# Twenty merge gates move from the attention into the merge, and the weight pieces get a fourth place

## The reference

```python
h = x * (1.0 + scale) + shift                     # ada: modulation from the condition
a_q, a_k, a_v, a_g, g_q, ..., s_u, s_v, s_g, m_a, m_g, m_s = split(h @ w_in)
y_attn = blocked_attention(q, k, v) * silu(a_g)   # softmax attention, 8 heads of 64
y_gla  = rms_norm(gla_scan(...) both ways) * silu(g_g)   # gated linear attention, 4 heads
y_sgu  = s_u * (w_s @ layer_norm(s_v) + b_s) * silu(s_g)
m = (sigmoid(m_a) * (y_attn @ w_br_attn)
     + sigmoid(m_g) * (y_gla @ w_br_gla)
     + sigmoid(m_s) * (y_sgu @ w_br_sgu))
x_new = layer_norm(alpha * x + gate * (m @ w_out))
```

## Time and profile before

| | us |
|---|---|
| median of 3 runs | 1342.85 (1341.75 to 1343.16) |
| profiled execution, whole | 1345.98 |
| span of the profiled execution, first to last instruction | 1344.1 |
| mean granted clock of PE in the profiled execution | 0.986 of full speed |

### The profile page before, as it was taken

The page is one execution under the profiler, slowest core; times in us unless marked ns, Lnnn a source line. Parts: engine busy times, 40 slices in busy tenths (PEclk is TensorE's granted clock), DMA queues, the critical chain, the costliest instruction groups (busy, mean ns, idle before and its releaser), DMA issues. The chain is left out here.

```text
span 1344.1 us, 19268 instructions
## 1 busy us (share of the span) xinstructions
PE 1299.5 (97%) x7922; PEld 990.2 (74%) x7922; DVE 625.0 (46%) x1096; ACT 552.3 (41%) x908; POOL 61.5 (5%) x88
## 2 busy tenths in 40 slices
PE   5999999999999999999999999999999999999996
PEld 2767778776778888878878889997767566666663
DVE  2313765576443352567476685767213252222212
ACT  2447433644663132346755568441344211111112
POOL 0000010232000000000000230000000000000000
PEclk7899999999999999999999999999899999999999
DMA  9523022235332341323432313553323869999990
GB/s 383 219 110 141 32 95 95 94 126 194 152 125 94 114 157 44 134 100 123 158 147 103 119 39 126 220 192 109 125 107 136 317 234 411 396 421 403 414 369 34
DMA packets 34653, 239.05 MB, mean 178 GB/s; under 512 B 4480, under 2 KB 4736, under 8 KB 6656
## 3 DMA queue, kind: packets, MB, share of 16 engines
q1 hardware_dynamic: 34560, 237.74, 45.5%
HBM read 236.68 MB, written 1.05 MB: 177 GB/s over the span
## 5 line engine op out<-in xcount | busy, mean ns | idle before, releaser
L231 DVE TENSOR_TENSOR pieces_lo<-weight_ring,pieces_hi 128x1024 fp32r<-128x1024 f32 x156 | 192.5, 1238 | 241.1 <-ACT pieces_hi L223 240.1
L249 PE MATMUL proj<-h_hi,pieces_hi 128*128 128x512 f32 (+1 forms) x800 | 284.7, 356 | 4.1 <-DVE pieces_lo L231 2.1
L251 PE MATMUL proj<-h_hi,pieces_lo 128*128 128x512 f32 (+1 forms) x800 | 276.1, 345 | 0.0
L250 PE MATMUL proj<-h_lo,pieces_hi 128*128 128x512 f32 (+1 forms) x800 | 274.7, 343 | 0.0
L223 ACT ACTIVATE pieces_hi<-weight_ring 128x1024 fp32r<-128x1024 f32 x156 | 163.5, 1054 | 147.2 <-PE score L251 96.1
L249 PEld LDWEIGHTS proj<-h_hi,pieces_hi 128*128 128x128 f32 x800 | 151.0, 189 | 31.6 <-issue 11.7
L250 PEld LDWEIGHTS proj<-h_lo,pieces_hi 128*128 128x128 f32 x800 | 151.4, 189 | 22.2 <-issue 2.9
L251 PEld LDWEIGHTS proj<-h_hi,pieces_lo 128*128 128x128 f32 x800 | 151.0, 189 | 19.8
L2042 PE MATMUL turn<-expert_parts,e_gathered 128*64 128x256 f32 x768 | 85.3, 379 | 0.8 <-DVE e_gathered L2234 0.8
L2042 PEld LDWEIGHTS turn<-expert_parts,e_gathered 128*64 128x64 f32 x768 | 56.0, 137 | 32.4 <-issue 7.3
L249 PE MATMUL score<-l_y_hi,pieces_hi 128*128 128x512 f32 (+1 forms) x192 | 65.3, 340 | 0.4 <-DVE l_merged L1416 0.2
(11 more groups left out here) (459 smaller groups left out, 2062.7 us busy)
## 6 DMA issues: line engine op xcount, KB each, us to landing
weight_ring<-in_stream SPq DMA_DIRECT2D x110, 1024.0 KB, 4.9
expert_parts<-in_experts SPq DMA_DIRECT2D x70, 1024.0 KB, 10.9
weight_ring<-in_experts SPq DMA_DIRECT2D x26, 1024.0 KB, 10.9
l_rows<-in_rows SPq DMA_DIRECT2D x2, 768.0 KB, 16.1
l_y_attn<-in_ada_first SPq DMA_DIRECT2D x1, 1024.0 KB, 5.3
l_y_gla<-in_ada_first SPq DMA_DIRECT2D x1, 1024.0 KB, 7.4
l_y_sgu<-in_ada_first SPq DMA_DIRECT2D x1, 1024.0 KB, 8.4
l_q<-in_ada_first SPq DMA_DIRECT2D x1, 1024.0 KB, 10.2
```

Of the source, the lines that this page charges most:

```text
L231: eng.tensor_tensor(self.part(self.lo_ring[:, n % NPIECE, :], kind), self.raw(slot, c, kind), self.part(self.hi_ring[:, n % NPIECE, :], ki ...
L249: pe.matmul(out, sh, mh, start=start, stop=False)
L250: pe.matmul(out, sh, ml, start=False, stop=False)
L251: return pe.matmul(out, sl, mh, start=False, stop=stop)
```

## The change

All 24 gates of both layers become `merge_gate` steps. The steps `early` and `sigmoids`, the buffer `early_gates` (14 KB per partition) and the raw copies are gone. `NPIECE` goes from 3 to 4, which takes 8 KB per partition. A `merge_gate` from the fifth cell on waits until the product four cells before has been read, as before for the cells after the early ones. Both order tables are new. Line numbers of the changed kernel are lower: L1106 becomes L1102, L1115 L1111, L1132 L1128, L1159 L1146 on ACT; L1283 becomes L1270, L1296 and L1297 become L1283 and L1284, L1344 and L1345 become L1331 and L1332, L1348 becomes L1335, L1359 becomes L1346, L1385 and L1386 become L1372 and L1373 on DVE. L223 and L231 stay.

```diff
-NPIECE = 3
+NPIECE = 4
...
-EARLY = (6, 14)
-EARLY_W = 3584
...
 ORDER_1 = """
...
-early.1 scale.3 early.2 score.4 pairs.2 early.3 early.4 pv.1 pairs.3 sums.3 diff.4 turn.3 early.5 diff.5 pv.2
-scale.4 scale.5 early.6 sums.4 pairs.4 early.7 diff.6 pairs.5 early.8 diff.7 scale.6 scale.7 turn.4 score.5
...
+diff.3 pairs.2 scale.3 pv.2 diff.4 turn.3 score.4 pairs.3 diff.5 mix.0 sums.4 scale.4 scale.5 pairs.4 pairs.5
+diff.6 diff.7 scale.6 scale.7 pv.3 pairs.6 diff.8 score.5 pairs.7 turn.4 diff.9 scale.8 scale.9 score.6 pairs.8
...
-                elif kind == "early":
-                    act.wait_ge(*PJ.ready(J("early", i)))
-                    act.activation(early_gate(i), PJ.tile(J("early", i))[:, 0:NT], ACT.Copy).then_inc(*PJ.evac(J("early", i)))
-                elif kind == "sigmoids":
-                    first, end = (0, EARLY[l] // 2, EARLY[l])[i:i + 2]
-                    for n in range(first, end):
-                        act.wait_ge(*PJ.evacuated(J("early", n)))
-                    gates = EG[:, first * NT:end * NT]
-                    act.activation(gates, gates, ACT.Sigmoid).then_inc(*sig.early_gates.one())
                 elif kind == "merge_gate":
                     b, c = i
                     n = "sag".index(b) * 8 + c
                     act.wait_ge(*PJ.ready(J("merge_gate", i)))
-                    if n >= EARLY[l] + 4:
+                    if n >= 4:
                         act.wait_ge(*PS.evacuated(J("br", "sag"[(n - 4) // 8], (n - 4) % 8)))
...
-                    if n < EARLY[l]:
-                        g = early_gate(n)
-                        dve.wait_ge(*sig.early_gates.at(1 if n < EARLY[l] // 2 else 2))
-                    else:
-                        g = SGM[:, n % 4, 0:NT]
-                        dve.wait_ge(*PJ.evacuated(J("merge_gate", i)))
+                    g = SGM[:, n % 4, 0:NT]
+                    dve.wait_ge(*PJ.evacuated(J("merge_gate", i)))
```

More of the change, by code:

```diff
@@ L438 @@
[L438 to L447, removed]
@@ new lines @@
+h.6 h.7 hsplit.2 hsplit.3 ag.0 gate.0 ag.1 ak.0 gq.0 stat.0 z.0 aq.0 z.1 gq.1 aq.1 stat.1 rstd.1 aq.2 ada.0.4
+stat.3 z.2 gk.0 rstd.0 z.3 stat.2 rstd.2 soft.0 aq.3 av.0 ag.2 vt.0 stat.4 decay.0 gk.1 decay.1 rot.2 rstd.3
+gv.0 gv.1 rot.3 rstd.4 rot.1 key.0 gv.2 rot.4 keymul.0 rot.0 gv.3 score.0 ag.3 sums.0 score.1 sg.0 keyt.0 key.1
+sv.0 keymul.1 sv.1 keyt.1 turn.0 score.2 kv.0 diff.0 sv.2 sums.1 sums.2 sv.3 svstat.0 scale.0 adat.0.4 turn.1
+svn.0 kv.1 score.3 kv.2 pv.0 sums.3 sg.1 pv.1 turn.2 score.4 turn.3 diff.1 diag.0 score.5 pairs.0 pv.2 pv.3
@@ new lines @@
+sums.4 turn.4 diff.2 score.6 scale.1 sums.5 diag.1 sums.6 sg.2 turn.5 pairs.1 scale.2 sg.3 diff.3 score.7
+scale.3 pairs.2 ada.0.5 diff.4 scale.4 pv.4 turn.6 pv.5 sums.7 sgsilu.0 score.8 su.0 pv.6 pairs.3 turn.7 diff.5
+adat.0.5 score.9 scale.5 ada.1.0 sums.8 pv.7 turn.8 pairs.4 diff.6 score.10 sums.9 turn.9 pairs.5 scale.6 su.1
+sums.10 mix.0 adat.1.0 diff.7 score.11 mix.1 scale.7 pv.8 turn.10 score.12 pairs.6 pairs.7 diff.8 scale.8 su.2
+sums.11 pairs.8 sums.12 diff.9 pv.9 su.3 diff.10 turn.11 scale.9 score.13 mix.2 mix.3 scale.10 pairs.9 ada.1.1
@@ new lines @@
+sums.13 pv.10 diff.11 pv.11 adat.1.1 ada.1.2 pairs.10 turn.12 score.14 diff.12 adat.1.2 scale.11 scale.12 pv.12
+sums.14 turn.13 pairs.11 ada.1.3 diff.13 score.15 adat.1.3 pairs.12 ada.1.4 scale.13 pv.13 fold.0 pairs.13
+adat.1.4 query.0 turn.14 turn.15 ada.1.5 sums.15 out.0 pv.14 silu.0 ostat.1 pv.15 gg.0 ysplit.s.0 ysplit.s.2
+gg.1 ysplit.s.1 ostat.0 out.1 silu.1 ostat.2 orstd.1 ostat.3 orstd.2 gg.2 orstd.0 gg.3 gated.0 ysplit.s.3
+gated.1 silu.3 silu.2 adat.1.5 orstd.3 merge_gate.s.0 gated.2 merge_gate.s.1 merge_gate.s.2 merge.s.0 merge.s.1
@@ new lines @@
+rot.4 rot.0 rot.2 rot.3 decay.0 decay.1 av.0 key.0 score.0 gv.0 gv.1 keymul.0 score.1 vt.0 gv.2 keyt.0 key.1
+gv.3 sv.0 sums.0 turn.0 score.2 keymul.1 sums.1 sv.1 keyt.1 sv.2 sv.3 diff.0 svstat.0 kv.0 scale.0 diff.1 pv.0
+svn.0 turn.1 kv.1 kv.2 diag.0 sums.2 diag.1 scale.1 pv.1 pairs.0 diff.2 scale.2 turn.2 score.3 pairs.1 sums.3
+diff.3 pairs.2 scale.3 pv.2 diff.4 turn.3 score.4 pairs.3 diff.5 mix.0 sums.4 scale.4 scale.5 pairs.4 pairs.5
+diff.6 diff.7 scale.6 scale.7 pv.3 pairs.6 diff.8 score.5 pairs.7 turn.4 diff.9 scale.8 scale.9 score.6 pairs.8
@@ new lines @@
+pv.4 sums.5 diff.10 turn.5 pairs.9 scale.10 diff.11 mix.1 pairs.10 turn.6 scale.11 pv.5 diff.12 sums.6 pairs.11
+score.7 scale.12 mix.2 diff.13 pv.6 turn.7 mix.3 pairs.12 scale.13 sums.7 gg.0 pairs.13 ysplit.s.1 query.0
+silu.0 silu.1 gg.1 pv.7 ysplit.s.0 merge_gate.s.0 ysplit.s.3 out.0 ostat.0 ysplit.s.2 out.1 ostat.1 ysplit.a.0
+ostat.3 ostat.2 orstd.0 gg.2 gated.0 orstd.2 gg.3 orstd.1 silu.3 gated.1 orstd.3 merge_gate.s.1 merge.s.0 silu.2
+gated.2 merge.s.1 merge_gate.s.2 gated.3 merge_gate.s.3 merge_gate.s.4 ysplit.a.1 merge.s.2 ysplit.a.2
@@ L480 @@
+merge.g.6 msplit.1 merge.g.7 msplit.2 final.0 msplit.3 final.1 final.2 final.3 final.4 finish.0 final.5 post_a.2
+post_b.2 tail.2 square.2 post_a.3 post_b.3 tail.3 square.3
 """
```

46 lines of the change are left out of this document (19 added, 27 removed).

## The result

The changed kernel takes 1355.22 us (median of 4, 1353.49 to 1356.31) against 1343.01 us for the kernel before (median of 4). The ratio is 1.0092, 95% interval 1.0073 to 1.0111. In a second comparison on another occasion it was 1.0085 (1.0068 to 1.0102). The change makes the kernel slower by about 12 us.

A forecast was written before the change was run, and what follows sets the result against it. PE was taken to bound the kernel, and DVE layer 1's attention once its gates go. Terms -2.5, +11.8 and +1.5 us sum to +10.8, forecast 1353.5 us at the median, range 1342 to 1365 at about 0.8.

The forecast's parts named there:

- The bound of the stretch: Layer 1's attention, last `sv` to `pairs.12`: without gates DVE bounds it, 47.1 us against PE's 35.3.
- What the profile was to show: Layer 1's attention: PE waits 10 us or more for `l_decayed`, about 47 us long, DVE 0.85 busy; trunk clock 1.00.
- The latency rival: Layer 1's attention: the levels' round trip bounds, not DVE's work; 57.8 us there, 1364 in all; chance 0.14.
- The clock rival: Layer 1's attention: new idle times lower PE's clock, up to +35 us, 1370 to 1390; chance 0.03.
- The gates in the merge: Layer 1's 14 moved gates take 2.88 us each instead of 2.98, -1.4 us; DVE and ACT keep up, 0.
- Layer 0: Six gates leave its attention: -1.1 us for cheaper gates, +1.5 us for a tight start of the attention; +0.4.
- The sum: Whole kernel: -2.5 for PE's own work, +11.8 for layer 1's attention, +1.5 for layer 0's; +10.8 us.
- layer 1's attention: Without its 13 gates it becomes DVE's, 47.1 us against PE's 35.3: +11.8 us, bounds +5.6 and +17.7.
- The fourth place: 0: Ring of weight pieces: PE hardly waits for pieces, so one more place is worth 0 to -2.8 us, taken as 0.
- The table loads: 0: Four more table loads on ACT, 5.2 us, lie beside PE's work: 0, at most 1 us.

The follow-up runs named there:

- experiment 5: Changed kernel with layer 1's masked copies on DVE covering 16 columns of 128: 1.0056 of the kernel before.
- experiment 8: Changed kernel with every masked copy of layer 1's levels done twice on DVE: 1.0167 of the kernel before.
- experiment 7: Changed kernel with layer 1's masked copies cut to 16 of 128 columns, exponentials and POOL's product to 64 of 256: 1.0067 of the kernel before.
- experiment 9: Changed kernel with 62 dummy PE matmuls at six idle times of layer 1's attention: 1.0075 of the kernel before.
- experiment 3: Changed kernel with NPIECE = 3 instead of 4: 1.0411 of the kernel before, 1399.18 us.
- experiment 10: Changed kernel with six of layer 1's gates back in its attention, at the longest idle times: 1.0071 of the kernel before.
- experiment 11: Changed kernel with six gates spread over the old order of layer 1's attention and three later gates between first merges: 1.0095 of the kernel before.

## Why the prediction was right, and where it was not

Forecast were 1353.5 us, 10.6 more than before; measured are 1355.22, 12.2 more.

**The bound of the stretch: right in the main.** Forecast 47.1 us from 40.95 us of DVE's work at 0.87; measured 46.9, 40.6 and 0.87. It is the experiments 5 and 8 that show it and not the agreement: DVE's work added or taken moves the stretch by 0.8 of it (8.2 of 10.3, and 2.6 of 3.2). "Bound by DVE" is not the whole. The remaining part of 0.2, the 1.9 us of the short exponentials and the quarter that the order of small steps costs say that DVE is not fed all the time, and experiment 7 says that DVE's work stops being the bound near 44 us. The idle 0.13 of DVE is an outcome of the order, not a constant of the engine: the runs without gates in the stretch have shares from 0.82 (experiment 7) to 0.92 (experiment 8). With these the forecast would have been 49.9 or 44.5 us, so that it met within 0.2 us is partly luck.

**What the profile was to show: partly wrong.** The prediction wanted 10 us or more of PE's waits at the matmuls for `l_decayed`. The list has 4.5 there (3.3 and 1.2), of 8.8 us of idle time; `diag`, the turns and the masked copies hold most of the rest, and 3.8 us of the excess are not waits at all. And the clock was to stay at 1.00 in the trunk.

**The latency rival: small.** Cutting the round trip gave 1.9 us of 12.6, and 0.6 us with the masks cut as well (44.3 to 43.7). It is DVE's work added in experiment 8 that rules it out as the pace of the changed kernel.

**The clock rival: it happened, and cost little here.** The prediction gave it 3% and up to 35 us. Its reason against it does not hold by its own rows: 35 of 47 us is 0.75, less than the 16.33 of 20 at the start. The clock fell twice, as the rows of experiment 9 show, and PE's slow matmuls lay mostly beside DVE's work: 0.6 us at least. The Trainium skill ("TensorE: Matmul & The Clock Gate", Part 1) says that activity releases the throttle; by that rule idle times bring the slow clock and dummies keep it away, and both traces agree. What it costs is another question, and depends on who bounds the stage: in layer 0 of experiment 3, where PE does, 6.9 of 26.0 us are longer matmuls.

**The gates in the merge: undersized.** -1.4 us for layer 1 was the price of the gate alone. The table shows -1.5 - 2.2 - 0.9 = -4.6 from `pairs.12` to the trunk's end, of which 13 x 0.10 is the gate's own; the rest is that merges with gates between them wait less (24 merge steps 34.5 us after, 35.4 before, in the timeline) and that the steps around them wait less too. Experiments 10 and 11 bear this out from the other side: without gates between the first merges the merge steps take 5.0 us more, and with three of them back 1.3.

**Layer 0: undersized.** +0.4 forecast, +3.4 measured (3.4 and 3.7 in two executions of the changed kernel; the runs with the same table of layer 0 and four places lie from +2.5 to +3.7). It is no cluster at the attention's start as I put it. PE's waits from 45 to 590 us sum to 4.4 us in ten places against 1.3 before, none over 1.1; the largest new ones:

```profile
PE turn L817 <- DVE modulation L1177: 0.9, 2, 0.7
PE turn L911 <- ACT l_decayed L1139: 0.7, 1, 0.7
PE proj L249 <- ACT l_gla_k L1038: 0.5, 1, 0.5
```

No run took layer 0's table apart.

**The sum: luck in part.** Against the forecast's terms, layer 0 is 3.0 us over and layer 1's attention 0.8 over, what follows `pairs.12` is 3.2 under, and the mixer and the experts, mostly by their clock, are 1.2 under. The misses nearly cancel, which is why the sum (+10.8) meets the profile's +10.3 better than its parts do.

**"The fourth place: 0".** As a term of the sum this held, for the changed kernel's PE waits 2.5 us for pieces, about as before. As a statement on what the place is worth ("0 to -2.8 us") it was wrong by more than any other: 44 us. The reasoning was that PE hardly waits for pieces before, so a place can't be worth more. But what a part is worth has to be asked with the other part in place. The new tables need it; the old ones run with three places and 2.1 us of such waits.

**The table loads: 0.** ACT waits 121.3 us at L1146 for `merge_gate`'s matmuls, so it has the time for four more loads there. No run isolates them.

## What to carry to other kernels

When independent filler work is taken out of a stretch, compute what is left there engine by engine: the stretch becomes about as long as the fullest engine's work divided by how full the order lets it be, however low that engine's share is over the whole kernel (DVE's was 46%). That second number is the weak one: it lay between 0.82 and 0.92 here. Filler helps only at the places where PE would idle: six gates at those places took 8.8 us of the excess away, six spread evenly 0.3. And a stretch with fewer of them elsewhere pays for it, so count both ends.

Ask of a fallen clock who bounds the stage before giving it a price. Where DVE set the pace it cost little, where PE did it cost all that the matmuls took longer.

Test the parts of a change together and apart. A ring's depth and an order written for that depth are one thing: each alone can cost several times what both together do.

## What the runs showed of the hardware

A masked copy on DVE takes 440 ns for 256 columns and 188 ns for 32, so by these two sizes an estimated third of it is fixed (152 ns), and shrinking such instructions buys far less than their columns say. PE's granted clock fell from 1.00 to 0.50 (the 1.2 GHz level) twice, behind idle times of 2.0 and 2.5 us and only when PE was busy again; with dummy matmuls in the idle times it stayed at 1.00. A gate of layer 1 that ran at a mean clock of 0.52 (experiment 11) took 5.46 us in place of 2.98. No list of waits shows this; only the window's clock and the longer rows do.
